# Adding up expert parts two at a time in every second turn, beside a decoder step's dense stages

## The chip, the cores and the metric

The kernel runs on one core of one Trainium2 chip. The metric is the device time of one execution in microseconds (us); the time given for a kernel is the median of its runs. The engines are called by their short names: PE (TensorE, matmuls; PEld is its weight load), DVE (VectorE), ACT (ScalarE), POOL (GpSimd), SP (SyncE, which issues DMAs).

## The reference

One layer of a decoder is computed for a prompt of 1024 tokens and 8 x 4 sample tokens, at model width 1024. Two token mixers (a gated linear recurrence, and dilated window attention) share one input projection; after them comes an expert mixer (`peer`), and that part is what the change touches:

```
q = rms_norm((xb @ wq).reshape(blk, P_HEADS, P_QDIM), qn_w)      # 8 heads
s1, s2 = scores of the two halves of q against 128 keys each
...                                                              # top 16 of each, top 16 of the 256 sums -> eidx, g
act = gelu(einsum('td,thkd->thk', xb, u[eidx]))
return einsum('thk,thkd->td', g * act, v[eidx])
```

For each token, 8 heads pick 16 of 16384 experts each. Each pick is a row of `u` (1024 floats, a dot product with the token) and a row of `v` (1024 floats, added up with the weight `g * gelu(dot)`). All of it is float32.

## The kernel before

The tokens are worked on in two halves ("_p": 512 prompt tokens; "_q": 512 prompt and 32 sample tokens). Each half passes through the dense stages one after the other, with a barrier of all engines (line 3191) behind each: norm, project, hgrn, attention, merge, branch, out, norm, query. The expert work is cut into 528 parts. One part is one pick (of 16) for 128 pairs of token and head, twice: two gathers of 128 rows of 8 KB (u and v together, 1 MB each), one for each of s = 0 and 1.

What happens to part p:

- POOL issues its two gathers into a slot of the ring (`fetch`, line 2928). The ring has 5 slots (`PART_SLOTS`), and a sixth for parts 33 to 125, beside the project stage of the second half. Before it issues, POOL waits until the part that had the slot before has been added up (`part_free`): that is part p-5, or p-6 while there are six slots. The plan puts the fetch of p into POOL's turn p-2 (p-3 with six slots).
- DVE multiplies the two u halves with the tokens and sums them to dots (line 3016, two instructions of 1.2 us), in its turn p. Before each it waits for that gather to land.
- ACT makes gelu and weights of the dots and scales two 128x64 patterns with them (`weigh`, lines 3046 to 3059, the last tile is `diag`). It does so in its turn p+1 while `lag` is 2. There are four `diag` buffers: the one of part p is free when part p-4 has been added up.
- PE adds the weighted v halves to the PSUM tile `expert_acc` (`sum_part`, line 3089): four float32 matmuls of 128x64 by 128x512, which stand in the trace as 8 MATMUL records. It does so in its turn p+2 while `lag` is 2, and waits for `diag_ready` first. The last of the four raises `part_free`.

Three things decide where turns fall. `Opening` (line 2601) runs the first 24 turns beside the query stage of the first half. `Beside` (line 2671) runs turns 24 to 256 beside the stages of the second half: every stage calls `beside.pe(cost)`, `beside.dve(cost)` and so on behind its units of work, the cost in us is added to that engine's `due`, and as many turns follow as have come due (`take`, line 2701). Each engine has its own count, in the order in which its instructions are written; nothing is reordered later. A place in the stage's code can so hold no turn, one, or several. `experts_rest` (line 3096) then runs the remaining turns alone, with `lag` set to 1: ACT weighs part i in its turn i, and PE adds up part i-1.

The stage's own work goes in the same in-order queues. In the project stage PE runs a unit of 8 to 32 matmul records (line 956 or 953), then its turns, then the next unit. In the query stage (line 2325) DVE takes its turns first and then copies a unit's result out of PSUM (line 2501); PE needs that copy one unit later, since it has two buffers with two pieces to a unit.

Of the kernel before, what the change touches and what calls it, by code (L numbers as in the profile page):

```python
# [149 lines left out]
class Modulation:  # L150
# [51 lines left out]
    def product(self, b):  # L202
        pe = self.nc.tensor
        pe.wait_ge(*self.loaded(b))
        at_least(pe, self.copied, b - 1)
        for c in range(DC):
            rows = slice(c % 4 * QUARTER, (c % 4 + 1) * QUARTER)
            ins = pe.matmul(self.acc[rows, b % 2, :], self.c_t[:, c, :], self.room(b)[:, c, :], start=(c < 4), stop=(c >= 4))
        ins.then_inc(self.product_done, 1)

    def fold(self, b):
        pe = self.nc.tensor
        pe.wait_ge(self.copied, b + 1)
        at_least(pe, self.row_ready, b - 1)
        pe.matmul(self.sum[:, b % 2, :], self.fold_rows[:, 0:MOD_ROWS], self.part[:, b % 2, :], start=True, stop=True).then_inc(self.sum_done, 1)
# [27 lines left out]
    def pe(self, t):  # L243
        if t < MOD_BLOCKS:
            self.product(t)
        if t - 1 >= MOD_FIRST and t - 1 < MOD_BLOCKS:
            self.fold(t - 1)
# [10 lines left out]
def opening_phase(nc, ph, span, const, x, modulation, in_weights, n_hi, n_lo, x_rows):  # L258
# [75 lines left out]

    @block.tensor
    def _(pe):
        pe.wait_ge(silu_done, 1)
        for c in range(DC):
# [2397 lines left out]
N_PARTS = N_GROUPS * TOPK  # L2736
# [23 lines left out]
class Experts:  # L2760
# [310 lines left out]


    def pe(self, i):
        while self.summed < min(i - self.lag + 1, N_PARTS):
            self.sum_part(self.summed)
            self.summed += 1

# [274 lines left out]
```

## Time and profile before

| | |
|---|---|
| runs of the kernel before | 4434.45 us (median of 3; 4428.72 to 4441.49) |
| profiled execution, span | 4435.7 us |
| PE busy | 3251.9 us (73%) |
| DVE busy | 2593.4 us (58%) |
| ACT busy | 1955.8 us (44%) |
| POOL busy | 1472.8 us (33%) |
| HBM traffic | 1377.25 MB read, 74.57 MB written |
| gathers | 1107.36 MB on queue 0 |
| chain that ended last, by engine | DMA (the gathers) 20% of the span, PE 4%, DVE 3%, ACT 3%; it begins near 3012 us |

The profiled execution's span is 1.25 us above the median of the runs. A busy PE is not a PE at its peak: its clock is granted by a throttle at 1.2 or 2.4 GHz, and the mean granted share is shown for a stretch as PEclk (1.00 is 2.4 GHz all the time, 0.50 is 1.2 GHz). The stages of the second half stand between these barriers, in us from the start: norm 1045.6 to 1093.4, project to 1818.8, hgrn to 2054.8, attention to 2341.7, merge to 2491.0, branch to 2593.6, out to 2691.9, norm to 2737.6, query to 3011.5. Then the rest of the expert parts runs alone to the end. The query stage of the first half, with the opening turns, is 801.4 to 1045.6.

### The profile page before, as it was taken

Reading aid. Unit: us, or ns where it says so; the run is one execution under the profiler, and the core shown is the slowest. Engines: PE = TensorE matmul, PEld = TensorE weight load, DVE = VectorE, ACT = ScalarE, POOL = GpSimd, SP = SyncE. Lnnn points to the kernel's source line nnn. Section 1 sums busy time; section 2 is a strip of 40 time slices with the busy share of each in tenths; the row PEclk is TensorE's granted clock in tenths of the full one; section 3 lists DMA queues with packets and bytes.
Section 4 is the critical chain, followed back from the end, with each engine's and each line's share of the span. In section 5 each row is a group of like instructions: output and inputs, shape, how many; then the busy total and the mean of one; then the engine's idle time right before and its main releaser. Section 6 shows DMA issues by size and latency. Waiting matters only on the chain. (4 is left out here: it accounts for less than half of the span.)

```text
span 4435.7 us, 46775 instructions
## 1 busy us (share of the span) xinstructions
PE 3251.9 (73%) x14243; PEld 1706.6 (38%) x14243; DVE 2593.4 (58%) x6557; ACT 1955.8 (44%) x6710; POOL 1472.8 (33%) x1175
## 2 busy tenths in 40 slices
PE   6998868874999999786754687985555555555556
PEld 4677754642543346444432454651111111111111
DVE  2362334476557745584646536656766766766774
ACT  2122431145457734483532225544545545545554
POOL 4543102352322233231212112223444444444443
PEclk8998889986999999787976898987867677777769
DMA  6533244389999999796999978889999999999998
GB/s 258 198 138 129 71 154 171 115 347 356 393 384 356 378 365 387 288 358 232 402 315 383 369 277 308 348 321 383 421 404 421 420 404 415 413 403 414 415 407 334
DMA packets 313374, 1447.75 MB, mean 326 GB/s; under 512 B 42913, under 2 KB 104257, under 8 KB 164770
## 3 DMA queue, kind: packets, MB, share of 16 engines
q0 software_dynamic: 152064, 1107.36, 62.4%
q1 hardware_dynamic: 146690, 330.19, 21.0%
q10 hardware_dynamic: 14368, 7.21, 0.6%
q8 instruction: 113, 1.85, 0.2%
q14 instruction: 139, 1.14, 0.1%
HBM read 1377.25 MB, written 74.57 MB: 327 GB/s over the span
## 5 line engine op out<-in xcount | busy, mean ns | idle before, releaser
L2928 POOL DMA_INDIRECT uv_ring<-in_peer_uv,pick_idx x1024 | 1134.5, 1108 | 2255.1 <-PE expert_acc L3089 1929.2
L3089 PE MATMUL expert_acc<-uv_ring,diag 128*64 128x512 f32 x3968 | 1263.8, 773 | 665.6 <-ACT diag L3059 629.4
L3016 DVE SCALAR_TENSOR_TENSOR uv_ring<-uv_ring,n_pairs 128x1024 f32<-128x1024 f32 x1024 | 1246.5, 1230 | 672.9 <-DMA uv_ring<-in_peer_uv,pick_idx 639.9
L3089 PEld LDWEIGHTS expert_acc<-uv_ring,diag 128*64 128x64 f32 x3968 | 293.8, 163 | 1519.5 <-ACT diag L3059 994.2
L3046 ACT ACTIVATE gelu_cube<-dots_now 128x2 f32<-128x2 f32 x528 | 105.6, 200 | 929.7 <-DVE uv_ring L3016 854.3
L3054 ACT ACTIVATE pick_weight<-gelu_tanh,pick_share 128x1 f32<-128x1 f32 x1056 | 350.8, 379 | 17.6
L3059 ACT ACTIVATE diag<-half_pattern,pick_weight 128x64 f32<-128x64 f32 x1024 | 300.4, 340 | 16.6
L956 PE MATMUL h_acc_q<-in_w_all_q,n_all_q 128*128 128x512 f32 x640 | 286.8, 601 | 0.0
L3049 ACT ACTIVATE gelu_tanh<-gelu_cube,dots_now 128x1 f32<-128x1 f32 x1056 | 253.3, 286 | 16.2
L3051 ACT ACTIVATE pick_share<-dots_now,pick_prob 128x1 f32<-128x1 f32 x1056 | 245.4, 280 | 0.0
L953 PE MATMUL h_acc_q<-n_all_q,in_w_all_q 128*128 128x272 f32 x896 | 218.0, 399 | 10.0 <-DMA in_w_all_q<-in_w_in 10.0
L953 PEld LDWEIGHTS h_acc_q<-n_all_q,in_w_all_q 128*128 128x128 f32 x896 | 168.1, 191 | 76.5 <-issue 32.5
L956 PEld LDWEIGHTS h_acc_q<-in_w_all_q,n_all_q 128*128 128x128 f32 x640 | 119.0, 191 | 163.6 <-issue 163.4
L3047 ACT ACTIVATE gelu_cube<-gelu_cube,gelu_a 128x2 f32<-128x2 f32 x528 | 156.0, 296 | 17.2
L2459 PE MATMUL peer_q_acc_q<-n_all_q,wq_raw_q 128*128 128x272 f32 x512 | 132.5, 421 | 19.9 <-DMA wq_raw_q<-in_peer_wq 19.3
L896 ACT COPY h_stage_q<-h_acc_q 128x272 f32<-128x272 f32 (+2 forms) x76 | 31.9, 420 | 252.9 <-PE h_acc_q L953 155.5
L147 POOL TENSOR_TENSOR in_w_lo_p<-in_w_p,in_w_hi_p 128x2048 fp32r<-128x2048 f32 x30 | 137.6, 4585 | 2.4
L956 PE MATMUL h_acc_p<-in_w_lo_p,n_hi_p 128*128 128x512 f32 x320 | 126.3, 395 | 12.0 <-DVE h_stage_p L930 12.0
L956 PE MATMUL h_acc_p<-in_w_hi_p,n_hi_p 128*128 128x512 f32 x320 | 125.3, 392 | 0.0
L956 PE MATMUL h_acc_p<-in_w_hi_p,n_lo_p 128*128 128x512 f32 x320 | 125.1, 391 | 0.0
L2459 PEld LDWEIGHTS peer_q_acc_q<-n_all_q,wq_raw_q 128*128 128x128 f32 x512 | 103.8, 206 | 43.8 <-DMA wq_raw_q<-in_peer_wq 20.3
L146 POOL CAST in_w_hi_p<-in_w_p 128x2048 fp32r<-128x2048 f32 x30 | 56.9, 1896 | 187.1 <-DMA in_w_p<-in_w_in 187.1
(457 smaller groups left out, 4784.8 us busy)
## 6 DMA issues: line engine op xcount, KB each, us to landing
in_w_p<-in_w_in SPq DMA_DIRECT2D x34, 1024.0 KB, 7.2
in_w_all_q<-in_w_in SPq DMA_DIRECT2D x17, 2048.0 KB
ada_w<-in_w_ada SPq DMA_DIRECT2D x10, 2048.0 KB, 8.8
uv_ring<-in_peer_uv,pick_idx POOLq DMA_INDIRECT x1024
past_keys_q<-in_past_keys SPq DMA_DIRECT2D x16, 1024.0 KB
past_rows_q<-in_past_values SPq DMA_DIRECT2D x16, 1024.0 KB
score_pair<-scores SPq DMA_DIRECT2D x66, 128.0 KB
wq_raw_p<-in_peer_wq SPq DMA_DIRECT2D x16, 512.0 KB, 5.7
```

Of the source, the lines that this page charges most:

```text
L147: pool.tensor_tensor(self.lo[b][:, c], self.raw[:, half], self.hi[b][:, c].bitcast(F32), ALU.subtract).then_inc(self.split_done, 1)
L953: ins = nc.tensor.matmul(acc[:, s, 0:k], w_part[b][:, c, at * P:(at + 1) * P], n_part[:, c, t0:t0 + k], start=start, stop=stop)
L956: ins = nc.tensor.matmul(acc[0:k, s, 0:WB], n_part[:, c, at * P:at * P + k], w_part[b][:, c, :], start=start, stop=stop)
L2459: ins = nc.tensor.matmul(acc[:, v % SLOTS, 0:n], w_part[:, u % 2, c, :], n_part[:, c, t0:t0 + n], start=(c == 0 and e == 0), stop=(c == DC ...
L2928: pool.indirect_dma_start(self.rows_of(part, s), None, self.x["peer_uv"][0], bass.IndirectOffsetOnAxis(ap=self.idx[:, q % 2, s, k:k + 1], ...
L3016: ins = dve.scalar_tensor_tensor(out=row, in0=row, scalar=1.0, in1=self.n2[:, tile % 2, s if tile < LAST_TILE else 0, :], op0=ALU.mult, op ...
L3047: link(act.activation(self.cube[:], self.cube[:], ACT.Identity, bias=self.const["gelu_a"][:], scale=GELU_B))
L3049: act.activation(self.tanh[:, s:s + 1], self.cube[:, s:s + 1], ACT.Tanh, scale=dots[:, s:s + 1])
L3051: ins = act.activation(self.share[:, s:s + 1], dots[:, s:s + 1], ACT.Copy, scale=self.prob[:, q % 2, k, s:s + 1])
L3054: ins = act.activation(self.weight[:, s:s + 1], self.tanh[:, s:s + 1], ACT.Identity, bias=self.share[:, s:s + 1], scale=self.share[:, s:s ...
L3059: ins = act.activation(self.diag[:, part % DIAGS, s, 0:pattern.shape[1]], pattern[:], ACT.Copy, scale=self.weight[:, s:s + 1])
L3089: ins = pe.matmul(self.acc[s * 64:(s + 1) * 64, c, :], self.diag[:, part % DIAGS, s, :], rows, start=first, stop=last)
```

## The change

```
     def pe(self, i):
-        while self.summed < min(i - self.lag + 1, N_PARTS):
+        ready = min(i - self.lag + 1, N_PARTS)
+        if self.lag > 1:
+            ready -= ready % 2
+        while self.summed < ready:
             self.sum_part(self.summed)
             self.summed += 1
```

Before, PE's turn i adds up part i-2 (while `lag` is 2). After, an even turn adds up nothing, and an odd turn i adds up parts i-3 and i-2. An even part is so added up one turn later, an odd part in the same turn as before. It holds for the 24 opening turns too, where `lag` is also 2. With `lag` 1 nothing is changed, except that the first turn alone finds one part more to add up (254, 255 and 256 where it was 255 and 256). No other engine's code is changed.

## Rows read from the trace of the kernel before

**Rows 1.** Busy time in each stage; columns: PE, PEld, DVE, ACT, POOL, PEclk, DMA share, GB/s
```profile
801.00:1045.00 244.00, 185.86 (x832) 122.66 (x832) 142.99 (x370) 83.95 (x273) 112.96 (x84) 0.86 0.74 281
...
1094.00:1819.00 725.00, 708.33 (x2968) 354.96 (x2968) 409.95 (x1190) 387.47 (x1375) 211.81 (x198) 0.99 0.96 371
1819.00:2055.00 236.00, 167.81 (x728) 98.19 (x728) 178.17 (x523) 141.08 (x371) 64.34 (x56) 0.72 0.80 294
2055.00:2342.00 287.00, 179.37 (x1540) 116.56 (x1540) 157.43 (x377) 133.18 (x453) 62.33 (x58) 0.83 0.94 347
2342.00:2491.00 149.00, 79.34 (x971) 42.76 (x971) 97.17 (x244) 40.80 (x160) 31.70 (x30) 0.72 0.96 383
2491.00:2594.00 103.00, 79.85 (x313) 53.97 (x314) 41.88 (x100) 30.89 (x84) 14.99 (x14) 0.88 0.87 320
2594.00:2692.00 98.00, 88.99 (x384) 60.54 (x384) 43.63 (x112) 22.27 (x83) 15.20 (x16) 0.97 0.73 263
...
2738.00:3012.00 274.00, 241.73 (x1138) 159.92 (x1140) 155.55 (x400) 128.10 (x433) 74.01 (x72) 0.92 0.86 333
```

**Rows 2.** Waits of PE in 1094 to 1819: in total, times, longest
```profile
PE h_acc_q L953 <- DMA in_w_all_q<-in_w_in: 10.0, 1, 10.0
```

**Rows 3.** Timeline of PE in the project stage: start us, us, instructions
```profile
1228.99 3.94 PE L953 MATMUL h_acc_q<-n_all_q,in_w_all_q 128*128 128x272 f32 x16
1232.85 1.94 PE L3089 MATMUL expert_acc<-uv_more_q,diag 128*64 128x512 f32 x8
1234.72 7.60 PE L953 MATMUL h_acc_q<-n_all_q,in_w_all_q 128*128 128x272 f32 x32
1242.25 1.94 PE L3089 MATMUL expert_acc<-uv_ring,diag 128*64 128x512 f32 x8
...
1510.70 3.65 PE L3089 MATMUL expert_acc<-uv_ring,diag 128*64 128x512 f32 x16
```

**Rows 4.** Waits of all engines in 1094 to 1819
```profile
POOL uv_ring L2928 <- PE expert_acc L3089: 406.2, 70, 14.5
...
DVE uv_ring L3016 <- DMA uv_ring<-in_peer_uv,pick_idx: 162.8, 78, 11.2
```

**Rows 5.** Waits of PE beside the opening turns, 896 to 1045
```profile
PE expert_acc L3089 <- ACT diag L3059: 16.9, 7, 5.6
```

**Rows 6.** Timelines of PE, POOL and DVE in the query stage, part 245
```profile
2885.94 1.94 PE L3089 MATMUL expert_acc<-uv_ring,diag 128*64 128x512 f32 x8
...
2895.51 1.94 PE L3089 MATMUL expert_acc<-uv_ring,diag 128*64 128x512 f32 x8
...
2888.16 0.94 POOL L2928 DMA_INDIRECT uv_ring<-in_peer_uv,pick_idx  x1 [2.11 <-PE expert_acc L3089]
...
2905.66 1.22 DVE L3016 SCALAR_TENSOR_TENSOR uv_ring<-uv_ring,n_pairs 128x1024 f32<-128x1024 f32 x1
2910.81 0.44 DVE L2501 COPY peer_q_t_q<-peer_q_acc_q 128x272 f32<-128x272 f32 x1 [3.12 <-PE peer_q_acc_q L2459]
```

**Rows 7.** Timelines of POOL and DVE in the query stage, part 236
```profile
2828.64 0.98 POOL L2928 DMA_INDIRECT uv_ring<-in_peer_uv,pick_idx  x1 [9.48 <-PE expert_acc L3089]
2829.93 0.94 POOL L2928 DMA_INDIRECT uv_ring<-in_peer_uv,pick_idx  x1 [0.30 <-issue]
...
2838.63 1.22 DVE L3016 SCALAR_TENSOR_TENSOR uv_ring<-uv_ring,n_pairs 128x1024 f32<-128x1024 f32 x1 [0.99 <-DMA uv_ring<-in_peer_uv,pick_idx]
```

**Rows 8.** Waits of PE in the query stage, 2738 to 3012
```profile
PE peer_q_acc_q L2459 <- DMA wq_raw_q<-in_peer_wq: 19.3, 4, 5.8
```

**Rows 9.** Timelines of PE and POOL, and one window, where the rest begins
```profile
3011.90 3.68 PE L3089 MATMUL expert_acc<-uv_ring,diag 128*64 128x512 f32 x8 [4.63 <-PEq L3191]
...
3012.51 0.94 POOL L2928 DMA_INDIRECT uv_ring<-in_peer_uv,pick_idx  x1 [17.27 <-POOLq L3191]
...
3015.85 0.94 POOL L2928 DMA_INDIRECT uv_ring<-in_peer_uv,pick_idx  x1 [1.16 <-PE expert_acc L3089]
...
3010.00:3015.00 5.00, 3.10 (x8) 0.86 (x8) 0.00 (x0) 2.60 (x10) 1.88 (x2) 0.50 0.24 44
```

## The prediction, made before the change was run

> **What bounds the kernel now.** I read the busy times by stage first [rows 1]. The change acts only where `lag` is 2: in the opening turns and in the second half's stages, about 896 to 3012 us. Behind 3012 the expert parts run alone, and nothing of their loop is edited. Of the stages, project is the longest (725 us), and PE is busy there for 708 us at a granted clock of 0.99: it is PE-bound. The waits of PE agree: the one wait over 10 us in that stage is for the first weights behind the barrier [rows 2]. In branch, out and query PE is busy for 78%, 91% and 88%. In hgrn (71%), attention (62%) and merge (53%) no engine is full; there the work goes in chains from one engine to the next. So PE time is worth its full price in project, nearly that in branch, out and query, and less elsewhere.
>
> Then the two sides of the expert loop in the project stage. POOL waits 406 us in 70 places for a part to be added up, that is for a free slot, and DVE waits 163 us for gathers to land [rows 4]. POOL stands at its next fetch all the time, so an addition that comes later makes a gather later at once. That is the way in which this change can cost.
>
> **Part 1: fewer changes between stage work and expert work on PE.** What does one such change cost? [rows 3] has it in start times. A project unit of 16 records with one part behind it: from 1228.99 to 1232.85 for the unit, 3.86 us, and to 1234.72 for the part, 1.87 us. A double unit of 32 records without a part in between takes 7.53 us (1234.72 to 1242.25). Two parts in a row last 1.71 us longer than one (3.65 against 1.94), so 1.87 + 1.71 = 3.58 us. Two units with a part behind each: 2 x (3.86 + 1.87) = 11.46. The same work with the parts together: 7.53 + 3.58 = 11.11. One place less is worth 0.35 us; the additions themselves are not fewer.
>
> How many places go? I counted in PE's timeline where a run of line 3089 stands between other matmuls. Before there are 85 in project (70 of one part, 14 of two, one across the barrier). After the change a place keeps work only if it holds an odd turn, thus an odd part of today: 50. In the same way 7 to 3 in branch, 8 to 4 in out, 24 to 18 in query, 21 to 13 in hgrn, 13 to 7 in merge, 19 to 10 in the opening, 10 to 5 in the two norm stages, and 12 to 12 in attention, whose places hold two parts or more. The sum is 199 to 122.
>
> - Project: 35 x 0.35 = 12.2 us, all on the path. Its bounds are 0 (if something else becomes the bound) and 12.2.
> - Branch and out: 8 x 0.35 = 2.8 us, taken whole. Query: 6 x 0.35 = 2.1 us, taken whole.
> - Hgrn: 8 x 0.35 = 2.8, half of it taken, 1.4 us, since PE idles there for 29% of the time. Merge and norm: 11 x 0.35 = 3.8 us, taken as 0; PE waits for other engines there, and that idle time hides them now.
> - Opening: 9 x 0.35 = 3.1 us, of which I take 1.0.
>
> Together -19.5 us; between 0 and -27 (77 x 0.35) if none or all of it is exposed.
>
> **Part 2: waits of PE for the weights.** An even turn no longer waits for `diag_ready`. In the opening such waits make 16.9 us in 7 places [rows 5]. But the odd turn still waits for its own part, which is ready at the same moment as before, so whatever PE gains in the even turn it mostly waits for in the odd one. I take 0 of it beyond the 1.0 above; the bounds are 0 and -8 (the even half).
>
> **Part 3: gathers that are issued later.** With five slots the gather of an odd part p needs part p-5, which is even and is added up one turn later than now. With six slots (project) it is the even p. Where both parts stand in one place, nothing moves.
>
> In project DVE reads its rows late or early without harm: half of the time it only stands and waits for the next landing [rows 4], its dots are used by ACT well behind that, and PE never waits for ACT in that stage. I price it at 0, with PE's wait list as the cover; if that cover is gone it costs what DVE is late in each pair.
>
> In the query stage DVE's turn stands ahead of the copy that PE needs. Take part 245 [rows 6]: part 240 is added up from 2885.94, and the gather goes out at 2888.16, 2.2 us behind. With the change part 240 waits for the turn of 241, at 2895.51, so the gather goes at 2897.7. How long does one take when nothing is ahead of it? Part 236 is such a case, since DVE was standing there [rows 7]: issued at 2828.64, its second half is used at 2838.63, 10.0 us later. Part 245's second half would be usable at 2907.7 and not at 2905.66: DVE is 2.0 us late. Its next stage work is the copy at 2910.81, ahead of which it idled 3.12 us; that hides it. Most of the 9.5 us of delay vanishes since the gather now queued behind others. Some of the 17 pairs in this stage find no such cover. I take 4 us: about a third of the pairs at 2 us, some of it hidden. The ends are 34 us (17 x 2.0, none covered) and -5 us: PE waits 19.3 us for its weights in this stage [rows 8], and a gather that starts later leaves the DMAs to them; a quarter of that is the most I would give.
>
> In attention and merge the same holds with more time between turns: 44 parts in 436 us against 36 in 274 us. I take 2 us, between -3 and 12. Behind the evened parts ACT waits one turn longer for a free `diag`, two turns ahead still; priced at 0, covered by PE standing one to two turns behind ACT.
>
> **Part 4: the start of the rest.** Behind the last barrier PE's first addition takes 3.68 us at the low clock, and the DMAs carry 44 GB/s from 3010 to 3015, while the first gather goes out at 3012.51 and the next at 3015.85, released by that addition [rows 9]. With the change part 254 is still open at the barrier, and the first gather needs it: it goes out when the next one does now, at 3015.85, 3.3 us later. From there on the gathers are the bound to the end (the chain that ended last, in the table), so 3.3 us is lost at the end. Bounds 1.9 (the high clock) and 3.7.
>
> **The sum.** -19.5 + 4 + 2 + 3.3 = -10.2 us. Against the profiled 4435.7 us that is a span of 4425.5 us; the median stands 1.25 us below the span, so 4424 us. A measurement of this kernel tells about 0.3%, 13 us, from no change; my likeliest value is just inside.
>
> **A rule against it.** The rows show clocks between 0.72 and 0.97 in hgrn, merge, branch and out [rows 1], a mix of the two levels, and 0.99 only where PE never stops. A place without a part leaves a longer hole in stages that have holes. The Trainium skill, page "TensorE: Matmul & The Clock Gate", section "Loop structure matters more than you think", says that a loop that keeps matmuls back to back stays at the high clock and one that waits between them falls to the low one. By that rule holes made longer would cost clock here; rival C prices it.
>
> **The rivals.**
>
> A, slower: late gathers hold PE. In the query stage DVE stands at a row that has not landed, the copy behind it is late, and PE's next unit waits. It decides from the point where a gather's 10.0 us behind the pair's addition [rows 7] end later than DVE's turn plus the idle time ahead of its next copy. For it: POOL waits on PE at nearly every fetch. Against it: the 3.12 us of cover and the queue in the example [rows 6]. Price 34 us in place of 4: -10.2 + 30 = +20 us, 4454 us.
>
> B, no gain in project: the DMAs are 0.96 busy there [rows 1], and the freed 12.2 us turn into a wait for weights. For it: that share. Against it: 371 GB/s there against 383 GB/s in merge, and PE waits once only [rows 2]. -10.2 + 12.2 = +2 us, 4436 us.
>
> C, clock: in query the granted share falls from 0.92 to 0.85, and its 241.7 us of PE work grow by 241.7 x (0.92/0.85 - 1) = 20 us. +10 us, 4444 us. For it: hgrn and merge are at 0.72 with more holes. Against it: two parts together also make a longer stretch of work.
>
> D, more: the places in all stages count, 27 us, and half of the opening's waits, with nothing lost but the start of the rest: -27 - 4 + 3.3 = -28 us, 4407 us. Against it: PE's idle time in merge and hgrn.
>
> That the change does not do what it says can be left out: `lag` is 2 in all those turns, and no other line reads the new value.
>
> **How the numbers follow.** My forecast has 0.50 (a third of it beyond -13 us), A 0.13, B 0.14, C 0.07, D 0.16. Faster by over 0.3%: 0.16 + 0.17 = 0.33. Slower: 0.13 and 0.06 of C and the tails, 0.20. Within 0.3%: 0.47. The range leaves out the lower half of D and the upper half of A: 4409 to 4449 us.
>
> **What would show it.** In the profile after: about 50 places of line 3089 in project, and a project stage 12 us shorter with PE still at 98%; the first gather of the rest about 3.3 us behind the barrier's old distance; DVE's wait for gathers in the query stage grown by no more than some 10 us, and PE without a wait for line 2501. A stage that grew (query above all) with PE waiting for DVE or at a lower clock would show A or C; a new PE wait for `in_w_all` in project would show B.

## The result, and the profile after

| | kernel before | kernel after |
|---|---|---|
| median of ten runs each | 4437.75 us (4426.7 to 4451.71) | 4465.6 us (4455.69 to 4477.12) |
| ratio after / before | | 1.006, 95% interval 1.0043 to 1.0076 |
| profiled execution, span | 4435.7 us | 4462.6 us |
| project / hgrn / attention | 725 / 236 / 287 us | 723 / 250 / 289 us |
| merge / branch / out | 149 / 103 / 98 us | 154 / 105 / 93 us |
| query / rest | 274 / 1424 us | 280 / 1428 us |

The change costs 0.6%, about 27 us (19 to 34 us by the interval). The forecast was 4424 us and the range ended at 4449, so the prediction was wrong. Four executions of the experiments below took 4774 to 8133 us at a lower granted clock (one of e8, one of e9, and two of the kernel before, taken beside e9 to e12 and e13 to e16); the ratios leave them out, the medians given for e8 and e9 count them.

First the same view as [rows 1]: busy time in each stage after; columns: PE, PEld, DVE, ACT, POOL, PEclk, DMA share, GB/s.

```profile
1095.00:1818.00 723.00, 699.31 (x2976) 360.47 (x2976) 410.29 (x1190) 387.86 (x1376) 211.57 (x198) 0.99 0.95 373
1818.00:2068.00 250.00, 164.25 (x728) 100.12 (x728) 178.64 (x523) 141.33 (x371) 64.17 (x57) 0.70 0.77 285
2068.00:2356.00 288.00, 182.06 (x1532) 121.21 (x1532) 157.82 (x377) 132.90 (x453) 63.10 (x58) 0.81 0.94 343
...
2615.00:2709.00 94.00, 87.18 (x384) 60.07 (x384) 43.82 (x113) 22.37 (x83) 15.47 (x16) 0.96 0.72 274
2754.50:3034.50 280.00, 246.93 (x1136) 164.67 (x1136) 156.33 (x400) 127.93 (x432) 75.35 (x72) 0.90 0.86 329
```

Two stages are shorter, and by less than the others are longer. In hgrn PE's busy time has not grown (167.8 to 164.3 us); its idle time, 68.2 us before, is 85.8. In query the idle time is nearly the same (33.3 us, before 32.2) and PE is busy for 5.2 us more, at a clock of 0.90 where it was 0.92.

PE's waits in project, against [rows 2], and the waits of DVE and PE in query, against [rows 8] (each: total, times, longest):

```profile
PE h_acc_q L953 <- DMA in_w_all_q<-in_w_in: 18.6, 1, 18.6
PE h_acc_q L947 <- issue: 7.6, 21, 1.0
```

```profile
DVE uv_ring L3016 <- DMA uv_ring<-in_peer_uv,pick_idx: 63.9, 37, 7.2
...
PE peer_scores_q L2479 <- DVE score_stage_q L2517: 22.8, 11, 4.0
PE peer_q_acc_q L2459 <- DMA wq_raw_q<-in_peer_wq: 5.9, 2, 5.0
```

In the kernel before, the view of project had the first row below for the gaps at line 947, and the two views of query the others, for DVE's gathers and PE's wait for DVE:

```profile
PE h_acc_q L947 <- issue: 5.9, 16, 1.0
...
DVE uv_ring L3016 <- DMA uv_ring<-in_peer_uv,pick_idx: 23.2, 18, 2.1
...
PE peer_scores_q L2479 <- DVE score_stage_q L2517: 6.4, 6, 3.3
```

PE waits 8.6 us longer for the first weights of project than in [rows 2], and the gaps at line 947 make 7.6 us in 21 places where they made 5.9 in 16. In query DVE stands nearly three times as long for gathers; PE waits 16.4 us more for DVE's score copies and 13.4 us less for its weights.

The start of the rest, against [rows 9]: PE's addition line is now 3092, the barrier's 3194. The barrier ends at 3034.57.

```profile
3035.03 6.05 PE L3092 MATMUL expert_acc<-uv_ring,diag 128*64 128x512 f32 x16 [4.19 <-PEq L3194]
...
3038.99 0.94 POOL L2928 DMA_INDIRECT uv_ring<-in_peer_uv,pick_idx  x1 [20.35 <-PE expert_acc L3092]
```

Part 254 is open at the barrier, and the first gather waits for its addition: it goes out 4.4 us behind the barrier, where it was 1.1 us (3012.51 against 3011.4).

### The profile page after: what moved, and what is told of

It is laid out like the page before. It is cut to its first block and busy times, and to the rows that moved or that the text cites. A ratio compares the mean times of both kernels' runs of the same rounds, so it can differ in the third digit from the quotient of the medians.

```text
span 4462.6 us, 46775 instructions
## 1 busy us (share of the span) xinstructions
PE 3249.8 (73%) x14243; PEld 1731.8 (39%) x14243; DVE 2596.1 (58%) x6557; ACT 1955.8 (44%) x6710; POOL 1488.4 (33%) x1175
## 5 line engine op out<-in xcount | busy, mean ns | idle before, releaser
L2928 POOL DMA_INDIRECT uv_ring<-in_peer_uv,pick_idx x1024 | 1150.4, 1123 | 2323.2 <-PE expert_acc L3092 2057.8
L953 PE MATMUL h_acc_q<-n_all_q,in_w_all_q 128*128 128x272 f32 x896 | 213.1, 397 | 18.9 <-DMA in_w_all_q<-in_w_in 18.6
```

The source lines that it names most:

```text
L953: ins = nc.tensor.matmul(acc[:, s, 0:k], w_part[b][:, c, at * P:(at + 1) * P], n_part[:, c, t0:t0 + k], start=start, stop=stop)
L2928: pool.indirect_dma_start(self.rows_of(part, s), None, self.x["peer_uv"][0], bass.IndirectOffsetOnAxis(ap=self.idx[:, q % 2, s, k:k + 1], ...
```

## The experiments

Two theories were tested. Theory L: an even part that is added up one turn later frees its slot later, its gather goes out later, and that costs. Its rival: PE's own order costs (two parts in one place, longer holes, a lower clock). The ratio given for a run is against executions of the kernel before that were taken beside it, whose medians lay between 4438.99 and 4446.67 us. Most experiments restrict the new rule to some turns i of PE, by one more condition:

```diff
-        if self.lag > 1:
+        if self.lag > 1 and 29 <= i < 128:
             ready -= ready % 2
```

The late gathers can also be had without the pairs. PE's turns stay as in the kernel before, and POOL waits in `fetch` for the part that follows an even one:

```diff
         if before:
-            pool.wait_ge(self.part_free, before[-1] + 1)
+            late = before[-1] % 2 == 0 and before[-1] < 254
+            pool.wait_ge(self.part_free, before[-1] + (2 if late else 1))
```

A single stage differs by several us from one execution to the next with the same instructions, so stage lengths below are means over all profiled executions in which the stage had, or hadn't, the feature in question; the counts are given. The runs were made in groups, on five chips; the differences named for hgrn, attention and query show also within each group that has executions of both kinds.

### Both kernels once more

> The kernel before once more, for the spread of a stage's length from one execution to the next. If the stages repeat within 2 us (project 725, hgrn 236, merge 149, query 274, rest 1424), the hgrn stage's 240 to 250 us in the kernels run so far is an effect. If hgrn or merge move by 4 us or more without any edit, differences of that size in one profile say nothing. DVE's idle time ahead of its rows in the query stage should be 20 to 27 us again.

> The changed kernel once more. If its hgrn stage is again near 250 us the 14 us there are the change's; if near 240 to 244 most of them were chance. The wait for the first weights of the project stage should again be 16 to 19 us (10 before), DVE's idle time ahead of its rows in the query stage 60 to 75 us, and the rest 1427 to 1429 us.

4436.86 and 4460.85 us. Project 729.8 and 729.2, hgrn 235.3 and 245.1, attention 283.3 and 292.7, query 274.2 and 282.6, rest 1425.3 and 1428.4 us; PE waits 10.1 and 18.5 us for the first project weights. The losses in hgrn, query and the rest came again, in hgrn 9.8 us against the 14 of the first pair. The 2.4 us gained in project in the first pair of profiles did not: that stage needs more executions.

### Late gathers alone

> PE adds one part in every turn as before; only POOL waits, ahead of each gather whose slot was freed by an even part, for the next part to be added up too, which is when the changed kernel lets it go. Theory L: the changed kernel's loss is all here, without the gain on PE: 25 to 45 us slower than before, hgrn 10 to 15 us longer, query 6 to 10. Theory C: the gathers have slack, and this is within 8 us of before in the whole, hgrn within 4 us.

> The kernel of e3 (late gathers in all stages, PE's turns as before) once more. Theory L: project 732 to 736, hgrn 239 to 250, attention 288 to 293, query 277 to 282, total 4451 to 4486. Rival (e3's total was chance): project 725 to 730, query 271 to 275, total below 4450.

The edit is the second diff above. 4466.17 us, 1.0067 of before (1.0044 to 1.009), and 4483.9 us in the single run of e16. PE adds up one part per turn as before, and the loss is there all the same: 27 us of median against the runs beside it, where the whole change costs 28. e16 has project 739.4, hgrn 258.2, attention 292.4 and query 280.6 us, e3 733.9, 239.7, 290.8 and 277.9. Project and hgrn of e16 are longer than was expected for it. So theory L carries the sign and the size of the result, within the some 10 us that these intervals leave; the two spans of one kernel (4449.3 and 4482.1 us) also say how far a single execution can be off, 18.5 us of it in hgrn. DVE and PE in e3's query stage, to be laid beside the rows of after; the line numbers of the expert code are one higher:

```profile
DVE uv_ring L3017 <- DMA uv_ring<-in_peer_uv,pick_idx: 72.7, 41, 5.8
...
PE peer_scores_q L2479 <- DVE score_stage_q L2517: 16.5, 9, 3.3
PE peer_q_acc_q L2459 <- DMA wq_raw_q<-in_peer_wq: 6.9, 2, 4.6
```

The rest is not among these losses: 1424.9 and 1423.9 us, as before, since this edit leaves part 254 where it was.

### Project alone, and all but project

> Parts are paired on PE only in turns 29 to 127, beside the project stage; everything else is as before the change. Theory G (fewer changes between stage and expert work are worth 0.35 us each, 35 of them in a PE-bound stage): the project stage behind its first wait for weights is 11 to 12 us shorter, and the whole 8 to 12 us faster than before. Theory B (the freed time turns into waits for weights): the project stage is 2 us shorter at most, and the whole within 3 us of before. In both the later stages are as long as before.

> Parts are paired in all turns with lag 2 except 29 to 127; the project stage is as before. All of the slowdown should be here. Theory L (gathers issued later hold DVE or the stages' own loads) and theory C (two parts in a row hold PE twice as long in stages that go in chains from engine to engine) both say 28 to 38 us slower than before, most of it in hgrn (14), query (6), merge and branch (7) and the start of the rest (3.5). If it is under 15 us slower, the project stage is where part of the time went, against the stage lengths of the changed kernel.

Turns 29 to 127: 4444.98 us, 1.0013 (0.9996 to 1.0029). All turns but these: 4471.16 us, 1.0065 (1.0043 to 1.0087). The rule in project brings nothing that the total shows (8 to 12 us less were expected), though its places fell from 85 to 50 as counted; the loss is in the other stages. e2 is 32 us above the kernel before beside it, within the 28 to 38 expected, though its hgrn has 240.4 us and not the 14 us more that were expected there. Over four executions with the rule and an undisturbed start (e1, e10, e13, e17; e10 and e17 keep 56 places) the stage takes 722.5 us, over eight without it 727.9, that is 5.4 us less. Behind PE's first wait, for the weights, the five executions with 50 places (e1, e13, after, e6, e4) take 708.1 us (704.4 to 713.3), the eight 717.9 (715.4 to 721.3): 9.8 us less. Where the rest of the 12.2 us went can be read at the sample units (line 947, 64 short matmuls). First before, then e1, at the same units, in PE's timeline:

```profile
1306.29 1.94 PE L3089 MATMUL expert_acc<-uv_ring,diag 128*64 128x512 f32 x8
1308.16 2.03 PE L947 MATMUL h_acc_q<-in_w_all_q,n_all_q 128*32 128x128 f32 x55
1310.54 0.42 PE L947 MATMUL h_acc_q<-in_w_all_q,n_all_q 128*32 128x128 f32 x4 [0.35 <-issue]
1311.28 0.45 PE L947 MATMUL h_acc_q<-in_w_all_q,n_all_q 128*32 128x128 f32 x5 [0.32 <-issue]
1311.66 7.13 PE L956 MATMUL h_acc_q<-in_w_all_q,n_all_q 128*128 128x512 f32 x16
```

```profile
1313.00 1.88 PE L947 MATMUL h_acc_q<-in_w_all_q,n_all_q 128*32 128x128 f32 x46
1315.91 0.39 PE L947 MATMUL h_acc_q<-in_w_all_q,n_all_q 128*32 128x128 f32 x2 [1.03 <-issue]
1317.32 0.67 PE L947 MATMUL h_acc_q<-in_w_all_q,n_all_q 128*32 128x128 f32 x16 [1.02 <-issue]
1317.92 5.35 PE L956 MATMUL h_acc_q<-in_w_all_q,n_all_q 128*128 128x512 f32 x8
```

And e1's windows there (the seventh value is the clock):

```profile
1315.00:1317.50 2.50, 0.57 (x9) 0.42 (x13) 0.17 (x2) 0.00 (x0) 1.00 (x2) 1.00 1.01 419
1317.50:1321.00 3.50, 3.50 (x20) 1.73 (x14) 2.14 (x9) 2.85 (x9) 0.00 (x0) 0.55 1.01 418
1321.00:1326.00 5.00, 5.00 (x12) 2.09 (x11) 4.86 (x14) 4.48 (x18) 0.00 (x0) 0.97 1.06 436
```

The unit takes 4.92 us and not 3.50, with two gaps of 1 us; behind them the clock stands near its lower level (0.55) for 3.5 us, which is 1.6 us of work lost. Together 3.0 us for one unit. In the eight executions without the rule the clock falls 3 times at sample units in all, in the seven with it (after, e6 and e4 too) 18 times. With 50 places and one fall (e13, after) the stage behind its first wait takes 706.8 and 704.4 us, 12.3 us less than 717.9, which is the forecast gain; with two (e4) 705.3, with four (e1, e6) 713.3 and 710.7 us.

The falls do not need the pairs. In e3 and e16 PE's order is as before and the gathers are late all through project; the clock falls there 2 and 3 times, and behind its first wait the stage takes 720.7 and 725.2 us. e3 has the same two gaps:

```profile
1613.03 0.44 PE L947 MATMUL h_acc_q<-in_w_all_q,n_all_q 128*32 128x128 f32 x6 [1.02 <-issue]
1614.49 0.47 PE L947 MATMUL h_acc_q<-in_w_all_q,n_all_q 128*32 128x128 f32 x8 [1.01 <-issue]
```

In e9, e11 and e2, without late gathers inside the stage, it falls 0, 1 and 1 times. So the falls seem to go with the late gathers, by two executions only. PE waited for nothing in these gaps that the profile shows ("issue"); what makes them was not tried.

### The start of project

> The new rule for turns 0 to 28 alone (the opening and the norm stage), all later turns as before. Theory L, that an addition that comes later holds back the gather behind it, and that such a gather then collides with the stage's own transfers: PE's wait for the first project weights is 16 to 19 us as after the whole change (18.6), not 10, project is 6 to 8 us longer than before and ends so, hgrn stays at 235 to 237 and query at 271 to 276; total 4444 to 4448. Rival (the wait for the weights is chance and comes with nothing): that wait is 9.5 to 10.5 us, total within 4 us of the kernel before.

> PE as in the kernel before; only POOL waits for one part more ahead of the gathers whose slot was held by an even part below 28, as it has to in the changed kernel. Theory L: PE's wait for the first project weights is 13 to 19 us. Rival (the pairs in PE's own queue make it, not the gathers): 9.5 to 10.5 us.

e9 restricts the rule to i < 29, e11 the late gathers to slots held by parts below 28.

e9: 4444.7 us, 1.0011 (0.9992 to 1.0031); project 734.4 us. e11, one run: 4448.69 us, project 729.3. The wait of PE for the first weights, e9 and then e11:

```profile
PE h_acc_q L953 <- DMA in_w_all_q<-in_w_in: 16.4, 1, 16.4
```

```profile
PE h_acc_q L953 <- DMA in_w_all_q<-in_w_in: 13.6, 1, 13.6
```

It is 9.6 to 10.3 us where the opening and norm turns and their gathers are as before. Late gathers alone make 3.6 us of the growth (e11; 3.3 and 4.2 in e3 and e16), with PE's turns untouched; where the opening's parts are paired too it is 16.2 to 18.6 us (e9, e4, e2, e6, after), so the gathers alone are not the whole of it. The last gather ahead of that barrier goes out 1.0 us before it in e11, 6.4 us in the kernel before, but 2.9 us in e9, whose wait is longer than e11's. In e9 part 26 is also left for project, one part more there (1.9 us). Five executions with a disturbed start and no pairs in project average 734.2 us (e9, e11, e2, e3, e16) against 727.9; without e3 and e16, which have late gathers inside the stage as well, it is 732.5. All of that lies in the first wait: behind it e9, e11 and e2 take 716.4 us. e11 by itself (729.3 us) lies within the spread of the eight (725.4 to 731.1).

### The barrier between project and hgrn

> PE as before; POOL waits for one part more only where the slot was held by part 120, 122 or 124, the last ones of project. Theory (a gather issued just ahead of the barrier makes hgrn's own first loads late): the last gather goes out 1 to 3 us ahead of the barrier and not 10, PE's longest wait for the turned keys in hgrn is 27 to 31 us (13 before), hgrn 239 to 243 us. Rival (it takes PE's pairs, or late gathers within hgrn): that wait 13 to 14, hgrn 235 to 238.

Late gathers for slots held by parts 120, 122 and 124 alone. One run, 4437.72 us; hgrn 240.8 us. POOL's timeline around the barrier at 1817.88, DVE's timeline behind it, and PE's waits in hgrn, all of e18:

```profile
1804.23 0.94 POOL L2929 DMA_INDIRECT uv_ring<-in_peer_uv,pick_idx  x1 [0.30 <-issue]
1817.35 0.94 POOL L2929 DMA_INDIRECT uv_ring<-in_peer_uv,pick_idx  x1 [12.18 <-PE expert_acc L3090]
1818.59 0.94 POOL L2929 DMA_INDIRECT uv_ring<-in_peer_uv,pick_idx  x1 [0.30 <-issue]
```

```profile
1844.89 1.37 DVE L1205 TENSOR_TENSOR_SCAN cum_q<-chunk_reset_q,logf_q 128x128 f32<-128x128 f32 x4 [13.74 <-DMA own_row_q<-c_own_row]
```

```profile
PE k_turned_q L1321 <- DVE e_k_q L1227: 30.0, 3, 27.8
```

The expected chain is there. In the kernel before the last gather ahead of this barrier was issued at 1808.99, 9.6 us before it; here one is issued at 0.5 us before it and its second half behind it. DVE then stands for a load of 1 KB, `own_row`, that SP issues at 1826.6, and PE's longest wait for the turned keys (`k_turned_q`) is 27.8 us where it was 13.1. A part of the longer stage is the barrier itself, in which the other engines stand until POOL has issued its gather: from the arrival of the others to their release it takes 2.0 us in e18, 1.9 in e3 and e16, 0.7 in the changed kernel and 0.3 in the kernel before. So the late gathers alone make more of this barrier than the change does, by 1.3 us (and in e3 and e16 as much again at the barrier ahead of query, 1.6 against 0.3 us).

The rows of the kernel before, from its POOL timeline and from PE's waits:

```profile
1808.99 0.93 POOL L2928 DMA_INDIRECT uv_ring<-in_peer_uv,pick_idx  x1 [0.30 <-issue]
...
PE k_turned_q L1321 <- DVE e_k_q L1227: 13.1, 1, 13.1
```

The same as in e18 shows in the changed kernel, in the timelines of POOL and DVE:

```profile
1816.05 0.94 POOL L2928 DMA_INDIRECT uv_ring<-in_peer_uv,pick_idx  x1 [11.44 <-PE expert_acc L3092]
1817.29 0.94 POOL L2928 DMA_INDIRECT uv_ring<-in_peer_uv,pick_idx  x1 [0.30 <-issue]
```

```profile
1845.44 1.37 DVE L1205 TENSOR_TENSOR_SCAN cum_q<-chunk_reset_q,logf_q 128x128 f32<-128x128 f32 x4 [15.73 <-DMA own_row_q<-c_own_row]
```

Over all profiles this is a clean mark: the longest wait for the turned keys is 27 to 31 us in the eight executions whose last gather is within 1 us of the barrier, 13 to 14 in the twelve where it is 9.5 us or more ahead. By itself it costs hgrn 4.5 us (240.9 us, e1 and e18, against 236.4 in nine executions with nothing late), less than the wait grew, as another one shrinks: from 1805 to 1880 us ACT waits 15.6 us for `q_in` in the kernel before and 2.9 us in the changed one.

The Trainium skill, page "DMA: Bandwidth & Descriptors", section "Queues, rings and completion order", says that a DMA engine takes turns between the queues that it has work for. The trace shows no turns, only the shares of the two queues: from 1805 to 1850 of the changed kernel the gathers' queue takes 57.9% of the DMA engines' time and SP's queue 28.9%, before 48.9% and 35.6%.

### Within hgrn

> Parts are paired only in turns 128 to 155, beside the hgrn stage. Theory C (two parts in a row hold PE 7 us at the low clock in a chain of engines) and theory L (late gathers) both say hgrn 4 to 14 us longer than before; DVE's idle time ahead of its rows there stays under 5 us by C and would have to grow by the loss under L. If hgrn stays at 236 to 240 us, the pairs in that stage cost nothing and its length in the changed kernel comes from what lies ahead of it. The rest of the kernel as before; the whole 0 to 14 us slower.

> PE as before; POOL waits for one part more where the slot was held by an even part from 126 to 152, the ones added up in hgrn. Theory L (late gathers): hgrn 239 to 242 us, DVE idle for gathers 2 to 5 us there. Rival (PE's pairs): hgrn 235 to 237.

> The new rule for turns 29 to 155: project and hgrn together. If what project leaves at the barrier and hgrn's own late additions add up: hgrn 244 to 250 us (before 235 to 237, either one alone 241), total 6 to 12 us above the kernel before. If they don't add: hgrn 240 to 242, total 0 to 6 us above.

e7 restricts the rule to turns 128 to 155, e13 to turns 29 to 155; e14 has late gathers for slots held by parts 126 to 153. e7: 4448.38 us, 1.0011 (0.9992 to 1.003), hgrn 240.8. e14, one run: 4448.22 us, hgrn 246.2, without any pair, 4 us beyond what was expected for it. e13: 4454.44 us, 1.002 (1.0002 to 1.0039), hgrn 244.4.

The late gathers inside the stage cost by themselves: 242.5 us (e7, e14, e2) against 236.4. Late inside and at the barrier: 247.0 us over six executions (239.7 to 258.2). 4.5 + 6.1 = 10.6, and the two do add up, in the means of executions that are up to 18.5 us apart. How the loss inside the stage comes about is only half seen: DVE's wait for gathers in it is 0 in the kernel before, 2.4 us in e7 and 4.7 us in e14, where the stage is 4.4 and 9.8 us above 236.4. e13's total of +0.2% has both and nothing else but project's gain.

### Query

> Parts are paired only in turns 221 to 255, beside the query stage. Theory L: DVE's idle time ahead of its rows grows from 26 to 60 to 75 us, the stage from 274 to 278 to 282 us, and with the open part 254 at the last barrier the rest is 3 to 4 us longer: 7 to 12 us slower than before in the whole. If L is wrong the stage is 2 us shorter (six changes between stage and expert work less) and the whole within 3 us of before.

> PE as before; POOL waits for one part more where the slot was held by an even part from 218 to 252, the ones added up in the query stage. Theory L: DVE's idle time for gathers there is 50 to 76 us (26.5 before), PE's wait for the copies that DVE makes grows from 6 to over 12 us, query is 277 to 281 us long. Rival (PE's pairs or the clock): query 271 to 275 with DVE idle or not.

e8: the rule for turns 221 to 255; e15: late gathers for slots held by parts 218 to 253. e8: 4443.53 us, 1.0005 (0.9985 to 1.0026), query 279.3. e15, one run: 4441.05 us, query 277.5, with these waits:

```profile
DVE uv_ring L3017 <- DMA uv_ring<-in_peer_uv,pick_idx: 68.1, 40, 7.3
...
PE peer_scores_q L2479 <- DVE score_stage_q L2517: 17.6, 11, 5.3
PE peer_q_acc_q L2459 <- DMA wq_raw_q<-in_peer_wq: 3.5, 1, 3.5
```

The late gathers alone give the picture of after: DVE stands, PE waits for its copies rather than for weights. Eight executions with late gathers in query average 279.6 us, twelve without 273.6. But PE's idle time is hardly part of it: 34.4 us on average against 33.2. PE's busy time is 245.3 against 240.3 us (after 246.9, e15 246.4, before 241.7). So the wait that moved costs by the clock rather than by its own length: by the traces' clock records 36.9 us of PE's busy time in the stage lie at 1.2 GHz with late gathers, 24.3 us without, and half of the difference, 6.3 us, is work lost. The stage's mean clock does not tell it (e15 has 0.92 as the kernel before, and 37.5 us at 1.2 GHz); it counts also when PE is idle. e8 by itself goes partly the other way (242.3 busy, 37.0 idle).

e8's total is not 7 to 12 us up, as was expected for it. A part of that expectation did not fit its edit: turn 256 is outside the new rule, so part 254 is not open at the barrier, and the rest takes 1424.8 us.

### Attention to out

> The new rule for turns 156 to 220 alone: attention, merge, branch and out. Theory L: DVE's idle time for gathers in attention rises from 8.5 to 25 to 32 us and the stage from 283-287 to 288-292 us; out falls from 98 to 91-93; project, hgrn and query as before; total between -3 and +6 us. Rival (these stages are free of it, and what was seen there comes from the state left by earlier ones): attention 283 to 287, out 98, total within 3 us of the kernel before.

Turns 156 to 220. 4444.52 us, 1.0007 (0.9989 to 1.0025). Attention 289.3, merge 153.9, branch 106.2, out 93.3 us. DVE's wait for gathers in attention is 26.1 us, as expected, where it was 7.4 before. Over all executions with and without the late gathers there: attention 290.7 against 284.2 (7 and 13), merge 151.1 against 152.5, branch 105.0 against 102.4, out 92.4 against 96.9 (7 and 12). Attention loses 6.5 us; out gains 4.5, also in e3 and e16 where PE has no pairs (92.8 and 92.7), so not by fewer places. Hgrn has 241.6 us in this profile, which nothing in the edit explains; it is the highest of the nine executions without a late gather.

### The last part taken alone

> The changed kernel, but turn 256, the last one beside the stages, adds up all that is ready, so that part 254 is not left open at the last barrier. The prediction's step on the start of the rest: the rest, from the last barrier to the end, is 3 to 4 us shorter than in the changed kernel (1424 in place of 1427.7 us), and the whole 3 to 4 us faster than it, so 22 to 25 us slower than before. If the rest's start has nothing to do with that part, the rest stays at 1427 us.

The rule for i < 256: turn 256 adds up part 254 ahead of the barrier, as before. 4458.27 us, 1.0043 (1.0025 to 1.006), somewhat nearer to the kernel before than the 22 to 25 us expected, but not by more than its interval. The rest takes 1425.7 us, as in the other sixteen executions that start it with part 255 (1423.5 to 1425.9); it takes 1427.7 to 1428.5 in the three that start it with 254. 3.3 us.

### Only where it paid

> The new rule for turns 33 to 119 alone, so that at the barriers ahead of and behind project the same parts are added up as in the kernel before. Theory L: PE's wait for the first weights is 10 us again, the saved places make project 7 to 12 us shorter than before (713 to 719), hgrn is 235 to 237 and not 241, total 6 to 12 us below the kernel before. Rival (what is saved in project is given back in hgrn whatever the state at the barrier): hgrn 240 to 241, total within 4 us of the kernel before.

> The new rule for turns 33 to 119 and 207 to 215 alone (the inner project stage, and out). If the gains seen in the stage lengths are real and independent: project 7 us shorter than before (717 to 724), out 92 to 94 us in place of 97, hgrn 235 to 238, query 271 to 278; total 8 to 12 us below the kernel before. Rival (out's gain needs the late gathers of branch ahead of it and is paid for there, and project's is within the spread): total within 4 us of the kernel before.

e10 restricts the rule to turns 33 to 119, e17 to these and 207 to 215. e10: 4436.97 us, 0.9999 (0.9982 to 1.0016); project 723.5, hgrn 235.4, PE's first wait 9.6 us. e17: 4439.45 us, 0.9994 (0.9976 to 1.0013); project 726.2, out 99.9 us. Both lose nothing, as theory L wants it, and neither is faster than the kernel before by what can be measured: the 6 to 12 and 8 to 12 us expected did not come, and in e17 the numbers are the rival's. The gain in out is gone when branch ahead of it is as before. By this one execution out lives on what branch's late gathers leave it, and pays there. In e17's project the clock fell at four sample units, in e13's at one (717.1 us).

## Why the prediction was wrong

By its own steps, in us. "Measured" is the difference of the means given above; for project, of the three executions with the rule in project and ahead of it (after, e6, e4) against the eight.

| step | predicted | measured |
|---|---|---|
| opening | -1.0 | 0.0 |
| project, 35 places | -12.2 | -11.1 behind PE's first wait (706.8 against 717.9); -9.8 with e1 and e13 |
| project, late gathers | 0 | +7.8 in PE's first wait (17.8 against 10.0), a part of it by pairs; in e3 and e16, without pairs, +5.0 behind it |
| hgrn, 8 places | -1.4 | |
| hgrn, late gathers | no term | +10.6 for both rows |
| attention and merge, late gathers | +2 | +6.5 - 1.4 = +5.1 |
| branch and out | -2.8 | +2.6 - 4.5 = -1.9 |
| query | -2.1 + 4 = +1.9 | +6.0 |
| start of the rest | +3.3 | +3.3 |
| sum | -10.2 | +19.8, with project as a whole at -3.3 (724.6 against 727.9) |

The medians differ by 27.9 us and the two pairs of profiles by 26.9 and 24.0. The 4 to 8 us that the table leaves over are not placed; hgrn alone was 250.0 and 245.1 in the changed kernel, where the table has 247.0.

**The step that failed** is Part 3, "gathers that are issued later", which put them at +6 us in all; by themselves they cost about 27 us (e3). It failed in two ways.

First, it followed a late gather to its own reader, DVE's row, and asked whether DVE had time. In project it had, but the 0 is not shown even for the middle of the stage: e3 and e16 are 5.0 us longer there, and in e10 the saved places would hide it. What the gather itself now runs beside was asked only in query, and as a gain. At both ends of project the late gather is issued just ahead of the barrier, where it was 6 to 10 us ahead, and the next stage's first loads then come late: +3.6 us of PE's wait for weights by gathers alone (e11), +4.5 us of hgrn (e18, e1). Rival B looked for weights that come late in project, but as a price of the freed time, and all along the stage; the wait came at its first instruction and had another cause.

Second, hgrn had no term for late gathers at all. I went from project to query to attention and merge, by where DVE's turn stands ahead of a copy, and gave hgrn only half of its places. It is one of the three stages whose work goes in chains from one engine to the next, and I had written so [rows 1]. Its late gathers cost 6.1 us within and 4.5 us from the barrier, the largest loss of all.

**Project's gain** was nearly the right size: 35 places went as counted, and where the clock fell once the stage behind its first wait is 12.3 us shorter (12.2 forecast). But the stage also has sample units, and there PE's gaps and then the clock take some of it back, 2.6 times a stage and not 0.4; with the longer first wait -3.3 us is left of the stage's gain. Falls of the clock are rival C in kind, which I had looked for in query and not in the stage with a clock of 0.99. "Only where PE never stops" was a wrong reading of that stage: PE has 16 gaps of 5.9 us in all at line 947 in the kernel before, and its clock fell once there already. The rule quoted from the Trainium skill (page "TensorE: Matmul & The Clock Gate", section "Loop structure matters more than you think") is about long waits for DMAs between matmuls. The trace agrees only in kind: here two gaps of 1 us with no wait stand ahead of the stretch at 0.55.

**Query** was rival A in kind, at a fifth of its price. Its late gathers made DVE wait 41 us more, well beyond the "some 10 us" that I named as the limit, and PE waited for DVE, though at line 2517 and not at 2501. The 34 us assumed that nothing gives way; in fact PE's wait for weights shrank from 19.3 to 5.9 us as that for DVE grew. I had taken that offset into the lower bound only. Rival C came there in kind too, and small: the clock is 0.90 where it was 0.92, not 0.85.

**Right** were the count of places (50 in project), the start of the rest to 0.1 us, and the sum for branch and out, though by other reasons than fewer places. The zero for diag waits came out by an exchange: in the opening they fell from 16.9 to 11.3 us, and PE's waits for DVE's score copies grew from 12.0 to 22.3.

**The chances.** A change with six small gains and a mechanism that makes a resource late at every second use got 0.20 for slower. The bounds of Part 3 (34 and 12 us) were wide enough to hold the result; my middle values were taken from the one example with cover.

## What to carry to other kernels

When a change frees a buffer later, follow the transfer that waits for it in two directions: to its reader, and to whatever shares the DMAs with it from its new start time on, above all the first loads behind the next barrier. Do so in each stage, the ones that look idle first: a chain of small steps has no cover, and a saving on the busiest engine counts only where that engine's clock and gaps stay as they are. Before such a change is costed, run the delay alone (one more count on the wait, the rest untouched); here that one edit had the loss but for the 3.3 us of the last barrier.

## What the runs showed of the hardware

- A load of 1 KB on SP's queue, issued at 1825.14 us behind a burst of gathers, was only used at 1845.44, when DVE had waited 15.73 us for it; in the kernel before the same load, issued at 1823.0, held nobody. SP stood 21.2 us in the issue of a 256 KB load at 1826.97, against 5.7 us for the same load before (1824.49).
- A run of 64 short matmuls (128x32 by 128x128) in e1 had two gaps of about 1.0 us in which PE waited for nothing that the profile shows, and the granted clock was at 0.55 for the next 3.5 us, with full-size matmuls already running.
- The barrier of all engines behind project lasted 2.0 us in e18 and 0.3 us in the kernel before. In e18 POOL was still issuing a gather (1818.59, 0.94 us long) when the others had arrived at 1817.9, and they went on at 1819.9.
- A first gather issued 3.3 us later at the start of the rest was seen in full in its length: 3.3 us in 1424, with the DMAs 0.99 busy in it.
- The same kernel (late gathers) had profiled spans of 4449.3 and 4482.1 us; the kernel before ran from 4420.01 to 4458.39 us beside e1 to e4.
